# Block attention in a fused fp32 kernel: row maxima in three parts, the first exponential ahead of ScalarE's copies, four probability buffers

## The chip, the cores and the metric

One Trainium2 chip; the program runs on one of its cores. Times are device microseconds (us) of one execution. The kernel before has a median of 3392.8 us over three runs (3386.49 to 3393.48).

## The reference, cut to what matters

The kernel computes two blocks of a network in fp32. Only the attention of the second block is touched by the change: 8 heads, 1024 queries, 1280 keys (256 of a context, 1024 of the sequence), 96 features a head, 64 values a head.

```python
def _block_attention(q, k, v):
    bn, L, H, dk = q.shape
    nb = L // Q_BLOCK
    scale = dk ** -0.5
    qb = q.reshape(bn, nb, Q_BLOCK, H, dk).transpose(1, 0, 2, 3, 4)

    def one(qi):
        s = jnp.einsum('bqhd,bkhd->bhqk', qi, k, preferred_element_type=jnp.float32) * scale
        p = jax.nn.softmax(s, axis=-1).astype(v.dtype)
        return jnp.einsum('bhqk,bkhd->bqhd', p, v)

    o = lax.map(one, qb)
    return o.transpose(1, 0, 2, 3, 4).reshape(bn, L, H * V_DIM)
```

The softmax subtracts the largest score of a row before the exponential; that largest score is what the change computes in another way.

## The kernel before

The function `attend` (L2440) runs in one stretch of the program, between the joint second block and the Fourier mixing. It goes through 32 steps `s`, four (`j` = 0 to 3) for each of 8 heads `h`. A step handles two tiles of 128 query rows, a and b, each with 1280 scores.

PSUM has eight banks of 512 fp32 columns. `pS` takes five: tile a lies in columns 0 to 1279 (sequence keys 0 to 1023 in banks 0 and 1, context keys in the first half of bank 2), tile b in columns 1280 to 2559 (context keys in the second half of bank 2, sequence keys in banks 3 and 4). Two banks, `pt`, are a ring through which everything else goes, and one, `pY`, sums probabilities times values.

The work of a step on each engine, each of which takes its instructions in the order of the program:

- **TensorE** (L2537 to L2640), `pair_scores(s)`: 18 products in three passes each (`scores`, L2555), first a's sequence keys, then the context keys of a and b, then b's sequence keys. The first part waits for exponential a of step s-1, the second for exponential b (`exped`). `scored` is raised twice, after the context part and at the end. Then, for step s-1, `turn_probs` (L2580) transposes the probabilities into the ring in five units t0 to t4 of four 128x128 transposes each; between and behind them come the value sums (`value_sums`, L2593) of two half steps before, four products at a time. At the end of steps j = 0 and 1 the two halves of the next head's queries are made (`make`, L2547), in step j = 2 its keys in three parts (L2552); step j = 3 makes nothing. A ring unit waits until the unit two places before it has been copied out (`wait_free`, L2513): t2 waits for the copy of t0, t3 for that of t1, t4 for that of t2.
- **ScalarE** (L2642 to L2711): copies t0 and t1 of step s-1 out of the ring (L2654), then the two exponentials of step s (L2695), each over 1280 scores with the row sums beside, then the high parts of the made queries or keys (`high`, L2657), and in every second step the copy of half of `pY` (L2706).
- **VectorE** (L2713 to L2813): two maxima over 1280 scores (L2781), one negation and scaling of both columns (L2783), the copies of t2, t3 and t4 (L2728), a reciprocal of both row sums behind exponential b (L2797), then `low` (L2731), which for a query half is five operations from the rotary product at L2739 to L2749, and in every second step the addition at L2808.
- **GpSimd** (L2815 to L2830): multiplies both tiles of probabilities by the reciprocals (L2823). TensorE's t0 waits for it (`normal`).

Steps j = 0 and 2 from the fifth step on end a half of a head's output. Where that head is the second of its pair, the half goes from VectorE's addition over GpSimd's gate (L2830) and ScalarE's copy (L2711) back to VectorE (L2812), in front of the next maxima. This happens in the four steps of heads h = 2, 4 and 6, which finish heads 1, 3 and 5; they are called the odd steps below, the others the even ones.

With three probability buffers (L2490) exponential b of step s goes to the buffer that t4 of step s-1 still reads:

```python
act.wait_ge(biased, s + 1)
if i >= 3:
    act.wait_ge(full, ring[("t", (i - 3) // 2, 4)] + 1)
```

Of the kernel before, what the change touches and what calls it, by code (L numbers as in the profile page):

```python
# [15 lines left out]
ACT = mybir.ActivationFunctionType  # L16
# [2423 lines left out]
def attend(nc, c, t, z, zk, x):  # L2440
# [40 lines left out]
    with Phase(nc, "attn") as ph:  # L2481
# [7 lines left out]
        r1, r2 = ph.sb("turned_cos", (P, HALF)), ph.sb("turned_sin", (P, HALF))  # L2489
        pr = [ph.sb(f"probs{j}", (P, T2)) for j in range(3)]  # L2490
        PT = [ph.sb(f"turned_probs{j}", (P, NKT, HALF)) for j in range(2)]
        yp, ytmp = ph.sb("attended", (P, SEQ)), ph.sb("odd_keys", (P, HALF))
        dg = ph.sb("gate", (P, 4, SEQ))
        mx, nb = ph.sb("max", (P, 2 * NS)), ph.sb("negated_max", (P, 2 * NS))
        sm, ri = ph.sb("sum", (P, 2 * NS)), ph.sb("inverse_sum", (P, 2 * NS))
# [29 lines left out]
        with nc.Block() as block:  # L2525
# [12 lines left out]
            def _(pe):  # L2538
# [24 lines left out]
                def pair_scores(s):  # L2563
# [7 lines left out]
                    scores(h, 2 * j, pS[:, 0:512], 0, 512)  # L2571
                    scores(h, 2 * j, pS[:, 512:1024], 512, 512)
                    if s:
# [6 lines left out]
                def turn_probs(n):  # L2580
                    _, s, i = n
                    o = wait_free(pe, n)
                    for kk in range(2):
                        k = 2 * i + kk
                        for ab in range(2):
                            if kk == 0 and i == 0:
                                pe.wait_ge(normal, 2 * s + ab + 1)
                            c0 = P * k if ab == 0 else (CTX + P * k if k < 8 else P * (k - 8))
                            mm = pe.transpose(o[:, 256 * kk + P * ab:256 * kk + P * ab + P],
                                              pr[(2 * s + ab) % 3][:, c0:c0 + P], c["ident"][:, :])  # L2590
                    mm.then_inc(full, 1)
# [51 lines left out]
            def _(act):  # L2643
# [13 lines left out]
                def high(n):  # L2657
# [7 lines left out]
                    else:  # L2665
                        c0, w = 512 * b, min(512, T2 - 512 * b)
                        act.activation(kh[h % 2][0:NOPE, c0:c0 + w], o[0:NOPE, 0:w], ACT.Copy).then_inc(highs, 1)

                act.wait_ge(landed[0], 80)
                for k in range(QT):  # L2670
# [10 lines left out]
                for s in range(NS + 3):  # L2681
                    if s == 0:
                        for n in values:
                            if n in by_act:
                                move(n)
                    for n in turned_at(s):
                        if n in by_act:
                            move(n)
                    if s < NS:
                        for ab in range(2):  # L2690
                            i = 2 * s + ab
                            act.wait_ge(biased, s + 1)
                            if i >= 3:
                                act.wait_ge(full, ring[("t", (i - 3) // 2, 4)] + 1)
                            act.activation(pr[i % 3][:, :], pS[:, T2 * ab:T2 * (ab + 1)], ACT.Exp, scale=scale,  # L2695
                                           bias=nb[:, i:i + 1], accum_out=sm[:, i:i + 1]).then_inc(exped, 1)
                    for n in made_at(s):
# [16 lines left out]
            def _(dve):  # L2714
# [61 lines left out]
                for s in range(NS + 3):  # L2776
                    if s < NS:
                        for ab in range(2):
                            i = 2 * s + ab
                            dve.wait_ge(scored, i + 1)  # L2780
                            ch.inc(dve.tensor_reduce(mx[:, i:i + 1], pS[:, T2 * ab:T2 * (ab + 1)], AX.X, ALU.max))  # L2781
                        dve.wait_ge(step, ch.n)
                        dve.tensor_scalar(nb[:, 2 * s:2 * s + 2], mx[:, 2 * s:2 * s + 2], -scale, None,  # L2783
                                          ALU.mult).then_inc(biased, 1)
                    if s == 0:
# [30 lines left out]
            def _(pool):  # L2816
                pool.wait_ge(gates_in, 64)
                for s in range(NS + 3):
                    if s < NS:
                        for ab in range(2):  # L2820
                            i = 2 * s + ab
                            pool.wait_ge(inverted, s + 1)
                            pool.tensor_scalar(pr[i % 3][:, :], pr[i % 3][:, :], ri[:, i:i + 1], 1.0, ALU.mult,  # L2823
                                               ALU.mult).then_inc(normal, 1)
# [383 lines left out]
```

## Time and profile before

| what | value |
|---|---|
| median of three runs | 3392.8 us |
| the profiled execution | 3391.3 us, span 3389.5 us |
| attention's 32 steps, first maximum to the end of the last value sums | 2821 to 3198 us of the span |
| mean time from a step's maxima to the next step's | (3173.94 - 2820.95) / 31 = 11.4 us |
| TensorE, VectorE, ScalarE, GpSimd busy, whole span | 93%, 59%, 28%, 4% |
| the same from 2900 to 3000 us | 90%, 69%, 46%, 26% |

The profile page gives busy shares for the whole span, where the large matrix products before attention fill most of it. What bounds attention is read from its own stretch: the waits there, and the timeline of single steps. TensorE's granted clock is given as a share of full speed: 1.00 is 2.4 GHz and 0.50 is 1.2 GHz.

### The profile page before, as it was taken

The page shows a single profiled execution, that of the slowest core. Times are in us where ns is not written, and L with a number is a line of the kernel's source. Part 1 is how long each engine was busy: PE and PEld are TensorE (multiplying, and loading weights), DVE is VectorE, ACT ScalarE, POOL GpSimd, SP SyncE. Part 2 cuts the span into 40 slices and gives each one's busy share as a digit, 9 for nine tenths or more (in the row PEclk, how much of TensorE's full clock was granted, in tenths as well). Part 3 has the DMA queues.
Part 4 walks back from the last instruction along what each step waited for, and adds up shares of the span by engine and source line. Part 5 has one row for each costly group of instructions (what it writes and reads, how often), then busy time and mean ns, then how long its engine had stood idle before and what let it go on. Part 6 is the DMA issues. An engine that isn't in the chain of part 4 may idle for free. (4 is left out here: it accounts for less than half of the span.)

```text
span 3389.5 us, 47701 instructions
## 1 busy us (share of the span) xinstructions
PE 3138.0 (93%) x20182; PEld 2905.0 (86%) x20182; DVE 1991.5 (59%) x2836; ACT 940.7 (28%) x1315; POOL 151.0 (4%) x124
## 2 busy tenths in 40 slices
PE   7999999998887999999999999999898977888787
PEld 7999999998876999999999998999898964555565
DVE  6666777664766455663574466444545526776446
ACT  5221222222444211211111112121323323444323
POOL 0000000000000000000000000000031001222200
PEclk9999999999988999999999999999898988999898
DMA  4223333333374344113213214111121330000121
GB/s 146 87 95 96 94 102 98 108 107 136 119 119 126 110 137 143 51 47 122 75 44 100 94 44 149 51 40 46 56 69 60 135 124 0 1 1 1 73 96 69
DMA packets 101822, 285.74 MB, mean 84 GB/s; under 512 B 13540, under 2 KB 32484, under 8 KB 100328
## 3 DMA queue, kind: packets, MB, share of 16 engines
q1 hardware_dynamic: 101608, 282.69, 26.1%
q8 instruction: 159, 2.61, 0.3%
q14 instruction: 55, 0.45, 0.0%
HBM read 218.79 MB, written 63.85 MB: 83 GB/s over the span
## 5 line engine op out<-in xcount | busy, mean ns | idle before, releaser
L471 PE MATMUL mixer_in_dense<-mix_z_high,mixer_in_whigh 128*128 128x348 f32 x1312 | 431.6, 329 | 15.3 <-DVE mixer_in_wlow L565 10.4
L471 PE MATMUL mixer_in_dense<-mix_z_high,mixer_in_wlow 128*128 128x348 f32 x1312 | 427.2, 326 | 0.0
L471 PE MATMUL mixer_in_dense<-mix_z_low,mixer_in_whigh 128*128 128x348 f32 x1312 | 426.4, 325 | 0.0
L1449 PE MATMUL flow_dense<-rst_norms_operand_b_high,flow_whigh 128*128 128x342 f32 x1248 | 399.5, 320 | 0.4 <-DVE flow_wlow L1542 0.4
L1449 PE MATMUL flow_dense<-irst_norms_operand_b_low,flow_whigh 128*128 128x342 f32 x1248 | 398.6, 319 | 0.0
L1449 PE MATMUL flow_dense<-rst_norms_operand_b_high,flow_wlow 128*128 128x342 f32 x1248 | 397.7, 319 | 0.0
L2012 PE MATMUL joint_dense<-rst_norms_operand_b_high,joint_whigh 128*128 128x342 f32 (+2 forms) x1056 | 344.6, 326 | 18.3 <-DVEq L2129 10.5
L2012 PE MATMUL joint_dense<-rst_norms_operand_b_high,joint_wlow 128*128 128x342 f32 (+2 forms) x1056 | 341.4, 323 | 0.0
L2012 PE MATMUL joint_dense<-irst_norms_operand_b_low,joint_whigh 128*128 128x342 f32 (+2 forms) x1056 | 340.4, 322 | 0.0
L1449 PE MATMUL flow_dense<-first_operand_a_high,flow_whigh 128*128 128x342 f32 (+1 forms) x912 | 291.6, 320 | 17.3 <-DVEq L1563 17.3
L1449 PE MATMUL flow_dense<-first_operand_a_low,flow_whigh 128*128 128x342 f32 (+1 forms) x912 | 292.1, 320 | 0.0
L1449 PE MATMUL flow_dense<-first_operand_a_high,flow_wlow 128*128 128x342 f32 (+1 forms) x912 | 291.4, 320 | 0.0
L471 PEld LDWEIGHTS mixer_in_dense<-mix_z_high,mixer_in_whigh 128*128 128x128 f32 x1312 | 251.6, 192 | 19.6 <-issue 16.9
L471 PEld LDWEIGHTS mixer_in_dense<-mix_z_low,mixer_in_whigh 128*128 128x128 f32 x1312 | 251.1, 191 | 0.0
L471 PEld LDWEIGHTS mixer_in_dense<-mix_z_high,mixer_in_wlow 128*128 128x128 f32 x1312 | 251.0, 191 | 0.0
L1492 ACT ACTIVATE flow_whigh<-first_norms_weights 128x1024 fp32r<-128x1024 f32 (+1 forms) x92 | 95.6, 1039 | 559.9 <-PE flow_dense L1449 536.9
L1449 PEld LDWEIGHTS flow_dense<-rst_norms_operand_b_high,flow_whigh 128*128 128x128 f32 x1248 | 235.3, 189 | 1.3 <-issue 1.2
L1449 PEld LDWEIGHTS flow_dense<-rst_norms_operand_b_high,flow_wlow 128*128 128x128 f32 x1248 | 235.2, 188 | 0.1
L1449 PEld LDWEIGHTS flow_dense<-irst_norms_operand_b_low,flow_whigh 128*128 128x128 f32 x1248 | 234.6, 188 | 0.0
L2012 PEld LDWEIGHTS joint_dense<-rst_norms_operand_b_high,joint_whigh 128*128 128x128 f32 x1056 | 202.0, 191 | 23.9 <-DVEq L2129 8.4
L2012 PEld LDWEIGHTS joint_dense<-rst_norms_operand_b_high,joint_wlow 128*128 128x128 f32 x1056 | 202.6, 192 | 0.6 <-issue 0.5
L2012 PEld LDWEIGHTS joint_dense<-irst_norms_operand_b_low,joint_whigh 128*128 128x128 f32 x1056 | 203.0, 192 | 0.0
(549 smaller groups left out, 5872.3 us busy)
## 6 DMA issues: line engine op xcount, KB each, us to landing
mixer_in_wstage<-w_in SPq DMA_DIRECT2D x56, 512.0 KB, 4.9
mixer_in_mod_w<-w_mod SPq DMA_DIRECT2D x64, 384.0 KB, 3.6
first_norms_weights<-w_up SPq DMA_DIRECT2D x44, 512.0 KB, 3.4
flow_side<-h SPq DMA_DIRECT2D x24, 512.0 KB, 5.1
h<-flow_out SPq DMA_DIRECT2D x24, 512.0 KB, 3.5
first_norms_weights<-ab_w_in SPq DMA_DIRECT2D x20, 512.0 KB, 3.5
p<-mixer_in_out SPq DMA_DIRECT2D x16, 528.0 KB, 2.8
first_norms_weights<-w_down SPq DMA_DIRECT2D x16, 512.0 KB, 3.8
```

The lines of the kernel that those rows point to most:

```text
L471: mm = pe.matmul(bank(s)[:, 0:W], a[n % 2][:, P * m:P * (m + 1)], z[x][:, m, W * b:W * (b + 1)], start=m == 0 and i == 0, stop=m == DT - 1 ...
L1449: mm = pe.matmul(o, w[n % NW][:, P * k:P * (k + 1)], x[h][:, k, where], start=k == 0 and e == 0, stop=k == kt - 1 and e == 2)
L1492: act.activation(wh[n % NW][:, 0:w], stage[n % 2][:, 0:w], ACT.Copy).then_inc(high_ready, 1)
L2012: mm = pe.matmul(pd[s % 2][:, 0:wide], a[n % 2][:, P * k:P * (k + 1)], m, start=k == 0 and e == 0, stop=k == DT - 1 and e == 2)
```

## The change

It is made in `attend` alone, in four parts.

1. `scored` is raised three times a step, so also after a's sequence keys (banks 0 and 1).
2. VectorE takes the maximum of a's 1024 sequence scores, then of both context parts in one instruction (2 x 256 scores into two columns of a new tile `context_max`), then joins, negates and scales for tile a; then the 1024 sequence scores of b, and the same for b. `biased` is raised once a tile instead of once a step.
3. ScalarE runs exponential a before its two copies of t0 and t1, and exponential b behind them.
4. There are four probability buffers, so both exponentials of step s wait only for t4 of step s-2.

```diff
-        pr = [ph.sb(f"probs{j}", (P, T2)) for j in range(3)]
+        pr = [ph.sb(f"probs{j}", (P, T2)) for j in range(4)]
...
-        mx, nb = ph.sb("max", (P, 2 * NS)), ph.sb("negated_max", (P, 2 * NS))
+        mx, mc, nb = (ph.sb(n, (P, 2 * NS)) for n in ("max", "context_max", "negated_max"))
...
-                    scores(h, 2 * j, pS[:, 512:1024], 512, 512)
+                    scores(h, 2 * j, pS[:, 512:1024], 512, 512).then_inc(scored, 1)
...
+                def exponential(s, ab):
+                    i = 2 * s + ab
+                    act.wait_ge(biased, i + 1)
+                    if s >= 2:
+                        act.wait_ge(full, ring[("t", s - 2, 4)] + 1)
+                    act.activation(pr[i % 4][:, :], pS[:, T2 * ab:T2 * (ab + 1)], ACT.Exp, scale=scale,
+                                   bias=nb[:, i:i + 1], accum_out=sm[:, i:i + 1]).then_inc(exped, 1)
...
+                    if s < NS:
+                        exponential(s, 0)
                     for n in turned_at(s):
                         if n in by_act:
                             move(n)
                     if s < NS:
-                        for ab in range(2):
-                            i = 2 * s + ab
-                            act.wait_ge(biased, s + 1)
-                            if i >= 3:
-                                act.wait_ge(full, ring[("t", (i - 3) // 2, 4)] + 1)
...
+                        exponential(s, 1)
...
                         for ab in range(2):
                             i = 2 * s + ab
-                            dve.wait_ge(scored, i + 1)
-                            ch.inc(dve.tensor_reduce(mx[:, i:i + 1], pS[:, T2 * ab:T2 * (ab + 1)], AX.X, ALU.max))
-                        dve.wait_ge(step, ch.n)
-                        dve.tensor_scalar(nb[:, 2 * s:2 * s + 2], mx[:, 2 * s:2 * s + 2], -scale, None,
-                                          ALU.mult).then_inc(biased, 1)
+                            dve.wait_ge(scored, 3 * s + 2 * ab + 1)
+                            c0 = (T2 + CTX) * ab
+                            ch.inc(dve.tensor_reduce(mx[:, i:i + 1], pS[:, c0:c0 + SEQ], AX.X, ALU.max))
+                            if ab == 0:
+                                dve.wait_ge(scored, 3 * s + 2)
+                                ch.inc(dve.tensor_reduce(mc[:, i:i + 2], pS[:, SEQ:SEQ + 2 * CTX].rearrange(
+                                    "p (a x) -> p a x", a=2), AX.X, ALU.max))
+                            dve.wait_ge(step, ch.n)
+                            dve.tensor_scalar(nb[:, i:i + 1], mx[:, i:i + 1], mc[:, i:i + 1], -scale, ALU.max,
+                                              ALU.mult).then_inc(biased, 1)
```

The indices of `pr` in the transposes and on GpSimd change from % 3 to % 4 with it.

On ScalarE, from the copies of a step that begins a head to the end of its third step (L2654 copies of t0 and t1, L2695 and in the change L2674 the exponentials, L2662 and L2664 the high parts of queries, L2667 those of keys), before:

```order
731 L2654 ACTIVATE attn_turned_probs<-attn_turned 128x2x256 x2
732 L2695 ACTIVATE attn_probs,attn_sum<-attn_scores,attn_negated_max 128x1280 x2
733 L2662 ACTIVATE attn_query_high<-attn_turned 64x512
734 L2664 ACTIVATE attn_query_high<-attn_turned_cos 32x512
735 L2654 ACTIVATE attn_turned_probs<-attn_turned 128x2x256 x2
736 L2695 ACTIVATE attn_probs,attn_sum<-attn_scores,attn_negated_max 128x1280 x2
737 L2667 ACTIVATE attn_key_high<-attn_turned 64x512 x2
738 L2667 ACTIVATE attn_key_high<-attn_turned 64x256
```

and with the change:

```order
734 L2674 ACTIVATE attn_probs,attn_sum<-attn_scores,attn_negated_max 128x1280
735 L2654 ACTIVATE attn_turned_probs<-attn_turned 128x2x256 x2
736 L2674 ACTIVATE attn_probs,attn_sum<-attn_scores,attn_negated_max 128x1280
737 L2662 ACTIVATE attn_query_high<-attn_turned 64x512
738 L2664 ACTIVATE attn_query_high<-attn_turned_cos 32x512
739 L2674 ACTIVATE attn_probs,attn_sum<-attn_scores,attn_negated_max 128x1280
740 L2654 ACTIVATE attn_turned_probs<-attn_turned 128x2x256 x2
741 L2674 ACTIVATE attn_probs,attn_sum<-attn_scores,attn_negated_max 128x1280
742 L2667 ACTIVATE attn_key_high<-attn_turned 64x512 x2
743 L2667 ACTIVATE attn_key_high<-attn_turned 64x256
```

The pair of copies stood ahead of both exponentials; now it stands between them.

On VectorE, a step's maxima and what follows them up to the reciprocal, before:

```order
1953 L2781 TENSOR_REDUCE attn_max<-attn_scores 128x1 x2
1954 L2783 TENSOR_SCALAR attn_negated_max<-attn_max 128x2
1955 L2728 COPY attn_turned_probs<-attn_turned 128x2x256 x3
1956 L2797 RECIPROCAL attn_inverse_sum<-attn_sum 128x2
1957 L2739 TENSOR_TENSOR attn_turned_sin<-attn_turned,attn_turn 32x512
```

and with the change:

```order
1965 L2786 TENSOR_REDUCE attn_max<-attn_scores 128x1
1966 L2789 TENSOR_REDUCE attn_context_max<-attn_scores 128x2
1967 L2792 TENSOR_SCALAR attn_negated_max<-attn_max,attn_context_max 128x1
1968 L2786 TENSOR_REDUCE attn_max<-attn_scores 128x1
1969 L2792 TENSOR_SCALAR attn_negated_max<-attn_max,attn_context_max 128x1
1970 L2732 COPY attn_turned_probs<-attn_turned 128x2x256 x3
1971 L2806 RECIPROCAL attn_inverse_sum<-attn_sum 128x2
1972 L2743 TENSOR_TENSOR attn_turned_sin<-attn_turned,attn_turn 32x512
```

Three instructions have become five, with the first negation behind the second of them; copies and reciprocal keep their places. TensorE's instructions keep their order.

## Rows read from the trace of the kernel before

**Rows 1.** Stretches: busy time (and instructions) of each engine, TensorE's clock, DMA.

```profile
core 0: us, PE busy (x) PEld busy (x) DVE busy (x) ACT busy (x) POOL busy (x), PEclk, DMA share, GB/s
2900.00:3000.00 100.00, 90.11 (x448) 53.67 (x447) 69.46 (x95) 46.04 (x76) 26.36 (x20) 1.00 0.00 1
```

**Rows 2.** Waits from 2822 to 3190: us in total, times, longest.

```profile
ACT attn_probs L2695 <- PE attn_turned L2589: 22.3, 14, 1.7
```

**Rows 3.** Groups by line and shape: busy us, mean ns, idle before.

```profile
L2781 DVE TENSOR_REDUCE attn_max<-attn_scores 128x1 f32<-128x1280 f32 x64 | 92.5, 1485 | 17.2 <-PE attn_scores L2559 16.7
...
L2728 DVE COPY attn_turned_probs<-attn_turned 128x512 f32<-128x512 f32 x96 | 63.3, 688 | 37.3 <-PE attn_turned L2589 37.2
```

**Rows 4.** Timeline, a step j = 1: start, duration, instruction [idle before].

```profile
2971.31 0.70 DVE L2739 TENSOR_TENSOR attn_turned_sin<-attn_turned,attn_turn 32x512 f32<-32x512 f32 x1 [1.25 <-PE attn_turned L2547]
...
2975.13 0.68 DVE L2808 TENSOR_TENSOR attn_attended<-attn_values_sum,attn_odd_keys 64x512 f32<-64x512 f32 x1
...
2975.74 2.87 DVE L2781 TENSOR_REDUCE attn_max<-attn_scores 128x1 f32<-128x1280 f32 x2
...
2976.88 1.09 PE L2589 MATMUL attn_turned<-all_ident,attn_probs 128*128 128x128 f32 x8
...
2977.90 1.08 PE L2606 MATMUL attn_values_sum<-attn_turned_probs,attn_values 128*64 128x512 f32 x4
...
2978.85 1.33 ACT L2695 ACTIVATE attn_probs<-attn_scores,attn_negated_max 128x1280 f32<-128x1280 f32 x1 [2.54 <-DVE attn_negated_max L2783]
...
2979.48 0.66 PE L2589 MATMUL attn_turned<-all_ident,attn_probs 128*128 128x128 f32 x4 [0.50 <-DVE attn_turned_probs L2728]
...
2980.07 1.99 PE L2547 MATMUL attn_turned<-attn_cq,attn_wq 128*128 128x512 f32 x4
...
2980.23 1.33 ACT L2695 ACTIVATE attn_probs<-attn_scores,attn_negated_max 128x1280 f32<-128x1280 f32 x1
...
2982.09 0.70 DVE L2739 TENSOR_TENSOR attn_turned_sin<-attn_turned,attn_turn 32x512 f32<-32x512 f32 x1 [0.25 <-PE attn_turned L2547]
...
2986.82 2.89 DVE L2781 TENSOR_REDUCE attn_max<-attn_scores 128x1 f32<-128x1280 f32 x2
```

**Rows 5.** Timeline, ScalarE's two copies and the exponential behind them.

```profile
2964.32 1.09 ACT L2654 ACTIVATE attn_turned_probs<-attn_turned 128x512 f32<-128x512 f32 x2 [3.59 <-PE attn_turned L2589]
...
2965.29 1.33 ACT L2695 ACTIVATE attn_probs<-attn_scores,attn_negated_max 128x1280 f32<-128x1280 f32 x1
```

**Rows 6.** Timeline, a step j = 3 and the start of the next head.

```profile
2997.51 2.89 DVE L2781 TENSOR_REDUCE attn_max<-attn_scores 128x1 f32<-128x1280 f32 x2 [0.57 <-PE attn_scores L2559]
...
3002.71 0.66 PE L2589 MATMUL attn_turned<-all_ident,attn_probs 128*128 128x128 f32 x4
...
3004.36 0.39 PE L2559 MATMUL attn_scores<-attn_key_low,attn_query_high 96*128 96x512 f32 x1
3004.94 0.38 PE L2559 MATMUL attn_scores<-attn_key_high,attn_query_high 96*128 96x256 f32 x1 [0.18 <-ACT attn_probs L2695]
...
3005.95 2.89 DVE L2781 TENSOR_REDUCE attn_max<-attn_scores 128x1 f32<-128x1280 f32 x2 [0.87 <-PE attn_scores L2559]
...
3007.88 0.98 PE L2589 MATMUL attn_turned<-all_ident,attn_probs 128*128 128x128 f32 x7 [0.47 <-POOL attn_probs L2823]
```

**Rows 7.** Timeline, a step j = 1 and a step j = 3, both odd.

```profile
3022.52 1.14 PE L2589 MATMUL attn_turned<-all_ident,attn_probs 128*128 128x128 f32 x8 [1.42 <-ACT attn_turned_probs L2654]
...
3022.74 2.89 DVE L2781 TENSOR_REDUCE attn_max<-attn_scores 128x1 f32<-128x1280 f32 x2
...
3046.77 2.89 DVE L2781 TENSOR_REDUCE attn_max<-attn_scores 128x1 f32<-128x1280 f32 x2
```

**Rows 8.** Timeline behind the last step: TensorE after its longest idle time in attention.

```profile
3183.07 0.44 PE L2589 MATMUL attn_turned<-all_ident,attn_probs 128*128 128x128 f32 x1 [3.28 <-POOL attn_probs L2823]
3184.29 1.75 PE L2589 MATMUL attn_turned<-all_ident,attn_probs 128*128 128x128 f32 x7 [0.77 <-POOL attn_probs L2823]
3185.97 1.98 PE L2606 MATMUL attn_values_sum<-attn_turned_probs,attn_values 128*64 128x512 f32 x4
```

**Rows 9.** Stretches, the same place, columns as in rows 1.

```profile
3183.00:3186.00 3.00, 2.16 (x10) 1.56 (x10) 0.00 (x0) 0.60 (x1) 1.23 (x1) 0.50 0.00 0
```

More of the change, by code:

```diff
@@ L2589, in turn_probs @@
                             mm = pe.transpose(o[:, 256 * kk + P * ab:256 * kk + P * ab + P],
-                                              pr[(2 * s + ab) % 3][:, c0:c0 + P], c["ident"][:, :])
+                                              pr[(2 * s + ab) % 4][:, c0:c0 + P], c["ident"][:, :])
                     mm.then_inc(full, 1)
@@ L2689, in _ @@
                     if s < NS:
-                        for ab in range(2):
-                            i = 2 * s + ab
-                            act.wait_ge(biased, s + 1)
-                            if i >= 3:
-                                act.wait_ge(full, ring[("t", (i - 3) // 2, 4)] + 1)
-                            act.activation(pr[i % 3][:, :], pS[:, T2 * ab:T2 * (ab + 1)], ACT.Exp, scale=scale,
-                                           bias=nb[:, i:i + 1], accum_out=sm[:, i:i + 1]).then_inc(exped, 1)
+                        exponential(s, 1)
                     for n in made_at(s):
@@ L2822, in _ @@
                             pool.wait_ge(inverted, s + 1)
-                            pool.tensor_scalar(pr[i % 3][:, :], pr[i % 3][:, :], ri[:, i:i + 1], 1.0, ALU.mult,
+                            pool.tensor_scalar(pr[i % 4][:, :], pr[i % 4][:, :], ri[:, i:i + 1], 1.0, ALU.mult,
                                                ALU.mult).then_inc(normal, 1)
```

## The prediction

> **What bounds the kernel now.** I read the stretches first, since only attention changes. From 2900 to 3000 us TensorE is busy 90 of 100 us at the full clock, VectorE 69 [rows 1]. So TensorE's idle time, about 10% of 353 us or 35 us, is the most that any reordering could win, and no engine is full: the steps are bound by a loop through several engines. The waits give one piece of it, ScalarE's wait for t4 of the step before, 22.3 us in 14 steps [rows 2], which is the buffer that the change adds. Whether that wait matters is read from the timeline of single steps.
>
> Measure a step from M, the start of its maxima. In a step j = 1, M is 2975.74 and VectorE came to it straight from other work [rows 4]. The loop is: exponential a at M+3.11; t2 and t3 on TensorE at M+1.14; four value products at M+2.16; t4 at M+3.74, late by 0.50 because VectorE's copy of t2 stands behind the maxima; the next query half at M+4.33; VectorE's `low` at M+6.35, with 0.25 of idle time for that query half; the next maxima at M+11.08, again with no wait for scores. The next M is set by `low`, and `low` by t4 and the query half. TensorE's scores are ready by then. Step j = 2 is alike, with keys in place of queries: its M is 2986.82, the next one 2997.51, where VectorE idled 0.57 [rows 4, 6]. Step j = 3 is bound by TensorE: VectorE idles 0.87 before 3005.95, and M to M is 8.44 [rows 6].
>
> So there are two kinds of step. In those that TensorE bounds, earlier maxima and exponentials can help. In those that VectorE enters late, ScalarE has its copies of t0 and t1 done long before M, and waits 2.54 for the negation [rows 4].
>
> **Maxima in parts.** 1280 scores take 1485 ns and a 512-wide copy from PSUM 688 ns [rows 3], so 768 more columns cost 797 ns: 1.04 ns each and 155 ns fixed. From M to exponential a are now 3.11 us, with 2560 columns, two reductions and a negation [rows 4]. After the change the way holds 1536 columns, two reductions and a negation: 1024 x 1.04 = 1.06 less, so M+2.05. For both tiles together VectorE gets one reduction (155 ns fixed) and one negation more, about 0.3 a step or 10 us in all. I cost that at nothing: it lies behind the first negation, and VectorE has nothing to copy until ScalarE has freed t2's bank, below. Were the cover gone, it would cost up to 10 us. The Trainium skill (VectorE: DVE Perf Modes, "The TRN2 errata") speaks against such a split, because many small tiles pay the fixed part each. Its table has 120 cycles at 0.96 GHz for an operation that reads PSUM and 58 for one that does not, an estimate of 0.19 a step and 6 us in all in place of 10.
>
> **The earlier signal.** The sixth score product ended at 3004.75 and the maxima began at 3005.95 [rows 6]. With a signal there the first maximum can begin at about 3004.79, 1.16 earlier, where VectorE is waiting. Where VectorE comes late it brings nothing.
>
> **ScalarE's order.** Now t2 must wait for: M, 2.05 to exponential a, 1.38 from one exponential to the next instruction (2978.85 to 2980.23 [rows 4]), the first copy. Two copies take 1.09, the next instruction starts 0.97 after the first, so one copy ends at 0.60 [rows 5]; with 0.04 for the hand-over t2 starts at 2.05 + 1.38 + 0.60 + 0.04 = M+4.07, not M+1.14. Then by rows 4: 1.02 for t2 and t3, 1.08 for the value products, 0.59 for t4, 2.02 from the query half to `low`: M+8.78, not M+6.35. `low` itself took 4.73 (2982.09 to 2986.82); where it does not run beside GpSimd it took 3.82 (2971.31 to 2975.13) [rows 4]. GpSimd would be nearly done by then, so I take 3.82: next M at +12.60, against 11.08.
>
> Step by step:
> - j = 1, seven steps: +1.52 each, 10.6.
> - j = 2: t4 and all behind it 2.43 later. Four even ones lose that less the 0.57 of idle time [rows 6], 1.86 each; three odd ones have no such idle time: 4 x 1.86 + 3 x 2.43 = 14.7.
> - j = 3, even: t4 at 4.07 + 1.02 + 1.08 = M+6.17; from t4 to the earlier signal are 3004.79 - 3002.71 = 2.08 [rows 6]: 8.25 in place of 8.44, -0.2 each, four times. Odd: VectorE enters late as in j = 1 (the one at 3046.77 [rows 7]), so t4 is 2.4 later and only the 1.16 comes off: +1.2, three times. Together 2.9.
> - j = 0, six steps (the first step of all is left as it is): the first maximum lies 1.16 nearer to the scores, while `low` keeps its place in TensorE's order; off come the wait for exponential b (0.18 of idle, 0.35 to 0.45 of delay) and about 0.4 of GpSimd's 0.47 [rows 6]. +0.3 each, 1.9.
> - The last head makes nothing; its steps are bound by TensorE and gain 0.2 to 0.5 each: -1.1.
>
> **The fourth buffer**: exponential b would start at 2.05 + 1.38 + 0.97 = M+4.40, and now starts at M+4.49 [rows 4, 5]. Its stall goes, but what comes late next is t4's copy, behind which the reciprocal stands. So nothing beyond the small gains above.
>
> Sum at a full clock: 10.6 + 14.7 + 2.9 + 1.9 - 1.1 = **+29 us**.
>
> **The clock.** TensorE would now be idle before t2. In j = 1 the gap is 4.07 - 1.14 = 2.93; in odd steps it grows from 1.42 by 4.07 + 0.22 to 5.7, three times [rows 4, 7]. Behind the last step TensorE idled 3.28 and 0.77, and the granted clock was then 0.50, the lower level [rows 8, 9]: seven transposes took 1.75 in place of 0.98, four value products 1.98 in place of 1.08 [rows 4, 6, 8]. A fall costs 1.7 us in these alone, and they are on the loop. The three long gaps surely pay it. Some 14 gaps of about 3 us are left. The stretch of [rows 1] stayed at 1.00 all along, and [rows 7] show that gaps of 1.42 occur now, the end of attention lost it behind 3.28 and 0.77; what I have to price lies between, so I take half of them. 10 x 1.7 = 17. Bounds: 3 x 1.7 = 5, and 17 x 1.7 = 29, or 36 at 2.1 if the work behind is slow too.
>
> **Forecast**: 29 + 17 = 46 us on 3391.3, the profiled execution, which is 1.5 below the median; on the median 3392.8 + 46 = 3439, with 3425 to 3452 as this case's own range.
>
> **Rivals.**
> 1. *The clock holds.* If gaps of 3 us do not lower it and the long ones hardly, the sum is 29: 3422, from 3412. For it: the gaps before odd t2 are at full speed now.
> 2. *The clock falls in every gap, and longer.* 29 + 29 to 29 + 36, rounded up for slow query products: 3451 to 3465. The Trainium skill (TensorE: Matmul & The Clock Gate, "HAM oscillation") describes this: a kernel whose matmuls came in bursts with waits between them fell back at every burst. [...] The fall at the end of attention agrees with it; no row of before has a gap of 2.9.
> 3. *Faster: TensorE bounds every step.* The late t2 would be absorbed if 4.71 us of work from t2 to `low` fitted in front of `low`'s other condition, exponential b and the reciprocal, at M+6.35; that decides at t2 = M+1.64. Then `low` keeps its time, and only the gains remain: 0.1 a step, and 0.5 to 0.9 in the dozen steps where TensorE waits for exponential b or GpSimd. That is -10, 3383. Against it: t2 cannot start before ScalarE has run an exponential that cannot start before M+2.
> 4. *No change.* Gains of rival 3 and a partial loss cancel, or ScalarE's copies are not on the path in most steps: within 7 us, 3393.
>
> **How the numbers follow.** About 0.2%, or 7 us, is what a measurement of this kernel can tell from no change. Forecast 0.48, rival 1 0.16, rival 2 0.20, rival 3 0.09, rival 4 0.07. Faster is rival 3, 0.09; same is rival 4, 0.07; slower the rest, 0.84. The range reaches from rival 1's lower end to rival 2's upper end, 3412 to 3465; rivals 3 and 4 are left out (0.16), and a little of both ends.
>
> **What would show it.** The waits after: TensorE's t2 on ScalarE's copy, near zero on TensorE now but for odd steps, should be the largest, some 2.9 a time. ScalarE's wait for t4 should be gone, and GpSimd's hold on t0 be shorter. Exponential a at M+2.05 and t2 at M+4.07 in every step. M to M: 12.6 in j = 1 and 12.5 in even j = 2 steps, 8.25 in even j = 3. The clock in stretches of 5 us behind long gaps tells between the forecast and rivals 1 and 2. Wrong would be: t2 ahead of exponential a's end, or j = 1 steps that keep 11.1 us.

## The result and the profile after

The changed kernel takes 3445.4 us (median of four runs, 3443.98 to 3449.6), the kernel before, timed beside it, 3390.0 us: a ratio of 1.0166, 95% interval 1.0148 to 1.0183, so 1.7% slower. The forecast was 3439 us and a loss of 46 us; the loss is 55.

The profiled execution of the change took 3449.6 us, the longest of its four. It entered attention 7.1 us later than that of before (the last activation of the stage ahead starts at 2772.20 against 2765.10), in code that the change does not touch; that is spread between executions. From there to the last subtraction of attention it took 487.0 us against 436.3: the change costs 51 us inside attention in these two traces.

Stretches, columns as in [rows 1]:

```profile
core 0: us, PE busy (x) PEld busy (x) DVE busy (x) ACT busy (x) POOL busy (x), PEclk, DMA share, GB/s
2900.00:3000.00 100.00, 84.22 (x392) 50.35 (x390) 60.68 (x97) 37.41 (x62) 23.70 (x18) 0.91 0.00 1
```

TensorE is busy 84 of 100 us where it was 90 [rows 1], although part of that work now runs at half the clock: the granted clock is 0.91 on average where it was 1.00. All other engines do less in the same time as well.

The waits in attention, us in total, times, longest:

```profile
ACT attn_probs L2674 <- DVE attn_negated_max L2792: 109.7, 31, 6.1
DVE attn_turned_probs L2732 <- PE attn_turned L2589: 87.0, 75, 2.3
PEld attn_turned L2589 <- ACT attn_turned_probs L2654: 84.3, 31, 6.6
PE attn_turned L2589 <- ACT attn_turned_probs L2654: 58.2, 18, 5.7
```

ScalarE no longer waits for t4, the 22.3 us of [rows 2]. In its place TensorE waits 58 us in 18 places for ScalarE's copies of t0 and t1, which stand behind an exponential that itself waits for the maxima.

Timeline of an even step j = 1, the same step s = 13 as in [rows 4]; start, duration, instruction [idle before]:

```profile
3000.25 1.21 DVE L2786 TENSOR_REDUCE attn_max<-attn_scores 128x1 f32<-128x1024 f32 x1
...
3001.38 0.67 DVE L2789 TENSOR_REDUCE attn_context_max<-attn_scores 128x2 f32<-128x512 f32 x1
3002.09 0.21 DVE L2792 TENSOR_SCALAR attn_negated_max<-attn_max,attn_context_max 128x1 f32<-128x1 f32 x1
...
3002.33 1.33 ACT L2674 ACTIVATE attn_probs<-attn_scores,attn_negated_max 128x1280 f32<-128x1280 f32 x1 [3.05 <-DVE attn_negated_max L2792]
...
3003.65 1.07 ACT L2654 ACTIVATE attn_turned_probs<-attn_turned 128x512 f32<-128x512 f32 x2
...
3004.29 1.60 PE L2589 MATMUL attn_turned<-all_ident,attn_probs 128*128 128x128 f32 x8 [2.83 <-ACT attn_turned_probs L2654]
...
3005.82 1.97 PE L2606 MATMUL attn_values_sum<-attn_turned_probs,attn_values 128*64 128x512 f32 x4
...
3007.72 0.88 PE L2589 MATMUL attn_turned<-all_ident,attn_probs 128*128 128x128 f32 x4
...
3010.36 0.69 DVE L2743 TENSOR_TENSOR attn_turned_sin<-attn_turned,attn_turn 32x512 f32<-32x512 f32 x1 [0.95 <-PE attn_turned L2547]
...
3014.37 1.23 DVE L2786 TENSOR_REDUCE attn_max<-attn_scores 128x1 f32<-128x1024 f32 x1
```

M is 3000.25. Exponential a starts at M+2.08 (it was M+3.11), so the maxima in parts do bring it forward by 1.03 us. The copies follow at M+3.40, and t2 starts at M+4.04, behind 2.83 us of idle time; it was M+1.14. Value products at M+5.57, t4 at M+7.47, `low` at M+10.11, the next maxima at M+14.12 against M+11.08.

The stretches around it show the clock fall:

```profile
3002.00:3004.29 2.29, 0.00 (x0) 0.00 (x1) 1.61 (x4) 1.96 (x4) 0.00 (x0) 1.00 0.00 0
3004.29:3007.72 3.43, 3.43 (x12) 1.43 (x13) 1.38 (x2) 1.74 (x3) 0.00 (x0) 0.58 0.00 0
3007.72:3012.00 4.28, 4.28 (x20) 3.06 (x19) 2.34 (x5) 0.59 (x1) 2.50 (x2) 0.94 0.00 0
```

In the gap it is still 1.00; in the 3.43 us after it, over t2, t3 and the value products, it is 0.58, so mostly 0.50, the lower level of 1.2 GHz. The products that take 1.08 us at full speed [rows 4] take 1.97.

### The profile page after: what moved, and what is told of

It reads as the page before. It is cut to its first block and busy times, and to the rows that moved or that the text cites. A ratio compares the mean times of both kernels' runs of the same rounds, so it can differ in the third digit from the quotient of the medians.

```text
span 3447.8 us, 47764 instructions
## 1 busy us (share of the span) xinstructions
PE 3164.5 (92%) x20182; PEld 2922.9 (85%) x20182; DVE 1997.8 (58%) x2900; ACT 935.3 (27%) x1315; POOL 151.0 (4%) x124
## 5 line engine op out<-in xcount | busy, mean ns | idle before, releaser
L2012 PE MATMUL joint_dense<-rst_norms_operand_b_high,joint_whigh 128*128 128x342 f32 (+2 forms) x1056 | 344.1, 326 | 19.4 <-DVEq L2129 10.5
L471 PEld LDWEIGHTS mixer_in_dense<-mix_z_high,mixer_in_whigh 128*128 128x128 f32 x1312 | 253.2, 193 | 19.5 <-issue 16.8
```

The source lines that it names most:

```text
L471: mm = pe.matmul(bank(s)[:, 0:W], a[n % 2][:, P * m:P * (m + 1)], z[x][:, m, W * b:W * (b + 1)], start=m == 0 and i == 0, stop=m == DT - 1 ...
L2012: mm = pe.matmul(pd[s % 2][:, 0:wide], a[n % 2][:, P * k:P * (k + 1)], m, start=k == 0 and e == 0, stop=k == DT - 1 and e == 2)
```

## The experiments

The theory: in the steps that VectorE enters late, ScalarE's copies of t0 and t1 behind exponential a hold t2, and with it everything up to the next maxima (29 us at a full clock); TensorE's idle time in front of t2 lowers the clock, which costs the rest. The rivals: the split maxima cost (by their fixed parts or by shared banks), the fourth buffer costs, or the order costs alike in every step. Nine kernels besides the change were timed. The kernel before was timed again beside them, with medians of 3389.9 us beside E1 to E4, 3391.9 beside E5 to E8 and 3388.5 beside E9, so small differences between runs of different groups are judged by the ratios.

| run | what | median us | ratio to before, 95% interval |
|---|---|---|---|
| E1 | the change with ScalarE's old order | 3385.0 | 0.9984, 0.9975 to 0.9994 |
| E2 | the new order alone | 3504.8 | 1.0345, 1.0328 to 1.0363 |
| E3 | four buffers alone | 3385.3 | 0.9986, 0.9978 to 0.9995 |
| E4 | maxima in parts alone | 3400.1 | 1.0029, 1.0016 to 1.0043 |
| E5 | the change, TensorE kept busy, fillers too long | 3444.2 | 1.0150, 1.0132 to 1.0168 |
| E6 | E1 and early copies in j = 2 | 3380.8 | 0.9970, 0.9958 to 0.9983 |
| E7 | E6 and late output halves | 3368.6 | 0.9930, 0.9916 to 0.9945 |
| E8 | the new order only where TensorE bounds | 3386.9 | 0.9984, 0.9973 to 0.9994 |
| E9 | the change, TensorE kept busy, fewer fillers | 3416.9 | 1.0083, 1.0052 to 1.0115 |

The time from a step's M to the next, read off the timelines as the difference of the starts of the first maxima (a cell stands for steps that agree within 0.1 us unless a range is given; steps 4 to 27):

| steps | before | forecast at full clock | change | E9 | E1 | E7 |
|---|---|---|---|---|---|---|
| j = 0 even | 13.9 | 14.2 | 14.20 | 14.20 | 14.19 | 14.2 to 14.6 |
| j = 0 odd | 16.8 | 17.1 | 17.05 | 17.06 | 17.04 | 14.31 |
| j = 1 even | 11.08 | 12.6 | 14.14 | 12.56 | 10.53 | 10.53 |
| j = 1 odd | 11.10 | 12.6 | 14.77 | 12.60 | 10.5 to 11.4 | 10.89 |
| j = 2 even | 10.69 | 12.55 | 13.8 to 14.0 | 12.46 | 10.4 | 9.9 |
| j = 2 odd | 12.9 to 13.0 | 15.4 | 16.9 | 15.32 | 13.3 to 13.4 | 9.85 |
| j = 3 even | 8.44 | 8.25 | 8.20 | 8.21 | 7.93 | 7.93 |
| j = 3 odd | 7.06 | 8.3 | 9.80 | 8.22 | 6.18 | 7.8 |

**E1: the old order back.**

```diff
-                    if s < NS:
-                        exponential(s, 0)
                     for n in turned_at(s):
                         if n in by_act:
                             move(n)
                     if s < NS:
+                        exponential(s, 0)
                         exponential(s, 1)
```

> The change without its part 3: ScalarE copies t0 and t1 ahead of both exponentials, as before; maxima in parts and four buffers stay. Theory (the order on ScalarE is the loss, and through it the clock): t2 starts again right behind the first value products, the clock stays at 1.00, M to M is about 11.3 in steps j = 1 (+0.3 from the longer maxima ahead of the copy of t2), and steps bound by TensorE gain 0.5 to 1; in all about 7 us under the kernel before, 3383. Rival A (the split maxima cost, in fixed parts or by sharing PSUM banks with TensorE and ScalarE): 10 to 50 us above before. Rival B (the fourth buffer or its place in SBUF costs): above before as well.

3385.0 us, 5 us under before and 60 under the change: with the old order the whole loss is gone, and both rivals, on maxima and on buffers, fall. The gain was a little smaller than expected, 5 us for 7, and it did not come where it was expected: even j = 1 steps took 10.53, not 11.3. The timeline of step s = 13 shows where the time went.

```profile
2978.76 1.21 DVE L2785 TENSOR_REDUCE attn_max<-attn_scores 128x1 f32<-128x1024 f32 x1
...
2982.85 0.65 PE L2589 MATMUL attn_turned<-all_ident,attn_probs 128*128 128x128 f32 x4 [0.84 <-DVE attn_turned_probs L2731]
...
2984.40 2.65 POOL L2831 TENSOR_SCALAR attn_probs<-attn_probs,attn_inverse_sum 128x1280 f32<-128x1280 f32 x2 [9.49 <-DVE attn_inverse_sum L2805]
...
2986.92 0.68 DVE L2744 TENSOR_TENSOR attn_turned_cos<-attn_turned_cos,attn_turned_sin 32x512 f32<-32x512 f32 x1
```

t4 is late by 0.84, more than the 0.50 of [rows 4], as the longer maxima ahead of its bank's copy would have it: M+4.09 against M+3.74. But GpSimd starts at M+5.64 and has 0.13 left, to M+8.29, when VectorE comes to the sum of the two rotary products at M+8.16. That operation, of which all operands lie in SBUF, takes 0.68 there. Before, it started at 2983.55, while GpSimd worked from 2981.94 to 2984.59, and took 1.58, to 0.54 behind GpSimd's end:

```profile
2981.94 2.65 POOL L2823 TENSOR_SCALAR attn_probs<-attn_probs,attn_inverse_sum 128x1280 f32<-128x1280 f32 x2 [9.15 <-DVE attn_inverse_sum L2797]
...
2983.55 1.58 DVE L2741 TENSOR_TENSOR attn_turned_cos<-attn_turned_cos,attn_turned_sin 32x512 f32<-32x512 f32 x1
```

The 0.90 saved here outweighs the 0.35 by which t4 is later: 11.08 + 0.35 - 0.90 = 10.53. In the table one odd j = 1 step of E1 took 11.4 instead of 10.5. In that step the granted clock fell, to 0.68 over 4.2 us from t4 on; in the two others it stayed at 1.00.

**E2: the new order alone**, on the kernel before, with its three buffers and whole maxima; the edit is that of the change's third part, with `biased` waited for at `s + 1` and the wait for t4 as before.

```diff
+                    if s < NS:
+                        exponential(s, 0)
                     for n in turned_at(s):
                         if n in by_act:
                             move(n)
                     if s < NS:
-                        for ab in range(2):
...
+                        exponential(s, 1)
```

> The kernel before with part 3 alone: exponential a ahead of the copies of t0 and t1, whole maxima, three buffers. Theory: exponential a at M+3.11, so t2 at M+5.1, about 1.1 later than in the change; exponential b then waits for t4, so the reciprocal and the next scores come late too. M to M about 15 in steps j = 1, 10 in steps j = 3; in all 80 to 100 us above before, about 3480: worse than the change, whose other parts soften it. Rivals A and B (maxima or buffers are the loss): within 7 us of before.

3504.8 us, 115 above before. The direction and the order of the runs are as the theory has it, but the loss is 15 us above the upper end of the expected 80 to 100. A step j = 1:

```profile
3021.10 2.87 DVE L2785 TENSOR_REDUCE attn_max<-attn_scores 128x1 f32<-128x1280 f32 x2
...
3024.21 1.33 ACT L2674 ACTIVATE attn_probs<-attn_scores,attn_negated_max 128x1280 f32<-128x1280 f32 x1 [4.07 <-DVE attn_negated_max L2787]
...
3026.17 1.92 PE L2589 MATMUL attn_turned<-all_ident,attn_probs 128*128 128x128 f32 x8 [3.86 <-ACT attn_turned_probs L2654]
...
3030.59 1.33 ACT L2674 ACTIVATE attn_probs<-attn_scores,attn_negated_max 128x1280 f32<-128x1280 f32 x1 [3.98 <-PE attn_turned L2589]
...
3032.30 2.65 POOL L2827 TENSOR_SCALAR attn_probs<-attn_probs,attn_inverse_sum 128x1280 f32<-128x1280 f32 x2 [14.13 <-DVE attn_inverse_sum L2801]
...
3033.70 1.79 DVE L2745 TENSOR_TENSOR attn_turned_cos<-attn_turned_cos,attn_turned_sin 32x512 f32<-32x512 f32 x1
```

Exponential a at M+3.11 and t2 at M+5.07 are as expected; exponential b is 3.98 late for t4. The estimate had counted neither the clock, which is granted at 0.51 in the 3.4 us behind this t2, nor the rotary sum beside GpSimd, 1.79 for 0.68. M to M is 16.05 to 16.08 in even j = 1 steps. So parts 1, 2 and 4 together save in this order: with them it costs 55, without them 115.

**E3: four buffers alone.** `range(3)` and all `% 3` become 4, and the wait is for t4 of step s-2.

```diff
-                            if i >= 3:
-                                act.wait_ge(full, ring[("t", (i - 3) // 2, 4)] + 1)
+                            if s >= 2:
+                                act.wait_ge(full, ring[("t", s - 2, 4)] + 1)
```

> The kernel before with part 4 alone: four probability buffers. Theory: exponential b starts at M+1.4 behind exponential a in every step, ScalarE's 22 us of waiting for t4 are gone, and with them TensorE's wait for exponential b and most of its wait for GpSimd in the steps it bounds, 0.8 to 1.2 us a head and some in the last head: 8 to 10 us under before, 3381. Rival (that wait is off the path): within 3 us of before.

3385.3 us, 5 us under before, where 8 to 10 were expected and 3 would have been the rival's. The buffer is worth half of the forecast. Even j = 3 steps take 8.0 in place of 8.44, and odd j = 0 steps 16.3 in place of 16.8; the even j = 0 steps win 0.46 in one head and 0.08 in two, and even j = 1 steps under 0.1. So the wait was on the path in steps that TensorE bounds, and not in all of them. The profiled executions show a second reason. All gains together are 5.1 us, but steps of the odd heads lost 1.8 us of it: odd j = 1 steps took 11.8, 11.7 and 11.1 where they had taken 11.1, and the j = 2 step behind the last of them 13.4 for 12.9. TensorE idles 1.42 us just ahead of such a j = 1 step and 1.82 in it, as before, but the clock stayed up before and fell here. Behind the second gap of step s = 9, before:

```profile
2934.44:2938.00 3.56, 3.56 (x13) 2.23 (x14) 2.31 (x5) 2.77 (x5) 1.09 (x1) 1.00 0.00 0
```

and in E3:

```profile
2934.40:2938.00 3.60, 3.60 (x9) 1.87 (x9) 1.40 (x3) 2.10 (x4) 1.20 (x1) 0.57 0.00 0
```

**E4: maxima in parts alone**, with three buffers and the old order.

```diff
-        pr = [ph.sb(f"probs{j}", (P, T2)) for j in range(4)]
+        pr = [ph.sb(f"probs{j}", (P, T2)) for j in range(3)]
...
-                    if s >= 2:
-                        act.wait_ge(full, ring[("t", s - 2, 4)] + 1)
+                    if i >= 3:
+                        act.wait_ge(full, ring[("t", (i - 3) // 2, 4)] + 1)
```

(against E1, with the indices of `pr` back at % 3)

> The kernel before with parts 1 and 2 alone: maxima in three parts, two negations, three buffers, old order. Theory: VectorE's extra 0.3 a step delays the copy of t2 in the 14 steps that it enters late, and the earlier signal brings little while exponential b waits for t4: 0 to 5 us above before, 3394. Rival A (the split maxima carry the loss): 20 us or more above before.

3400.1 us, 10 above before: worse than the 0 to 5 of the theory, well short of its rival. From its waits:

```profile
ACT attn_probs L2674 <- PE attn_turned L2589: 47.1, 31, 1.7
```

This is the wait of [rows 2], now in all 31 steps: exponential a ends earlier, and exponential b still has to wait for t4. By steps, the loss sits mainly in j = 0, 1.0 us each (14.9 even, 17.7 odd), and 0.35 in even j = 1; from step 4 on even j = 2 and all j = 3 steps are 0.3 to 0.7 shorter. With the fourth buffer (E1) the j = 0 steps take 14.2 and 17.0, so 0.7 of the 1.0 goes with the buffer's wait and only the rest can be VectorE's extra work. With the buffer the split makes no difference in time, 3385.0 us (E1) against 3385.3 (E3). VectorE's extra work can be read from the change's trace: the three reductions have means of 1220, 679 and 1220 ns and the negations 214 each, 3.55 us together against 2 x 1.485 + 0.17 = 3.14 before. That is 0.41 a step, more than the 0.3 that the prediction took, and more than double the 0.19 that it worked out from the table of the Trainium skill (VectorE: DVE Perf Modes, "The TRN2 errata"); the page's point, that many small tiles pay the fixed part each, stands.

**E8: the new order only where TensorE bounds.**

```diff
+                    ahead = s % 4 == 0 or s >= NS - 4 or (s % 4 == 3 and s // 4 % 2)
+                    ahead = ahead or s // 4 == 0 and s % 4 == 3
-                    if s < NS:
+                    if s < NS and ahead:
                         exponential(s, 0)
                     for n in turned_at(s):
                         if n in by_act:
                             move(n)
+                    if s < NS and not ahead:
+                        exponential(s, 0)
```

> The changed kernel with exponential a ahead of the copies only in the steps that TensorE bounds (all j = 0, even j = 3, the last head), and behind them in the 17 others. Theory: the loss sits in the others only, so this is E1 plus 0 to 3 us, about 3386, M to M 14.2 in j = 0 and 8.2 in even j = 3 as in the changed kernel, 10.5 in j = 1. Rival (the order costs in every step alike): a third to a half of the loss stays, 3405 to 3420.

3386.9 us, by the ratio the same as E1. Even j = 3 steps take 8.20 as in the change, 0.27 more than in E1, and even j = 0 steps 14.20 as in both. So all but some 2 us of the harm is done in the 17 steps that VectorE enters late, and the new order helps in none of the others.

**E5: TensorE kept busy in the gaps.** A zero matrix times the values is added to the running sum in `pY`, which leaves it as it is.

```diff
+                def keep_busy(s):
+                    if s < 4 or s >= 28:
+                        return
+                    odd = (s // 4) % 2 == 0
+                    n = {0: 0, 1: 10 if odd else 5, 2: 5, 3: 5 if odd else 0}[s % 4]
+                    for k in range(n):
+                        pe.matmul(pY[0:VD, :], zero[:, :], V[:, k % NKT, :], start=False, stop=False,
+                                  skip_group_check=True)
...
                         if n[2] % 2 and H is not None:
                             value_sums(H, pairs[n[2] // 2:n[2] // 2 + 1])
+                        if n[2] == 1:
+                            keep_busy(s)
```

> The changed kernel with extra value products of a zero matrix (they add 0 to the running sum, so the result stays) on TensorE in the gap in front of t2: 5 in steps j = 1 and 2 and odd j = 3, 10 in odd j = 1, none elsewhere. They fill most of a gap but not all. Theory (the clock falls in these gaps, and that is the part of the loss above the 29 us): granted clock near 1.00 in attention, M to M back to 12.6 in even j = 1, 12.5 in even j = 2, 8.3 in odd j = 3; 20 to 25 us under the changed kernel, about 3422. Rival (the excess has another cause, such as shared PSUM banks): M to M stays 14.1 and 14.0, and the time is that of the changed kernel or more.

3444.2 us, hardly a gain: taken by itself, the outcome of the rival. The stretches and the timeline say that it is not.

```profile
3000.00:3100.00 100.00, 98.14 (x434) 53.00 (x433) 60.92 (x97) 36.81 (x61) 20.65 (x16) 1.00 0.00 1
```

```profile
3003.82 1.21 DVE L2800 TENSOR_REDUCE attn_max<-attn_scores 128x1 f32<-128x1024 f32 x1
...
3004.86 4.45 PE L2601 MATMUL attn_values_sum<-attn_values,attn_zero 128*64 128x512 f32 x10
...
3009.25 1.09 PE L2591 MATMUL attn_turned<-all_ident,attn_probs 128*128 128x128 f32 x8
```

The clock stayed at 1.00, but a filler takes not the 0.5 us that I had planned with but 0.86 (two matmuls at 0.43 each), so five of them held t2 to M+5.43. From there on the step ran at full speed: 13.89 is the 12.6 of the theory and 1.3 of too long a filler. The fillers were too many, and E9 repeats the experiment with fewer.

**E9: fewer fillers.**

```diff
-                    n = {0: 0, 1: 10 if odd else 5, 2: 5, 3: 5 if odd else 0}[s % 4]
+                    n = {0: 0, 1: 6 if odd else 3, 2: 3, 3: 3 if odd else 0}[s % 4]
```

> As E5 with fewer fillers. One took 0.86 us on TensorE, not the 0.5 that E5 was laid out for, so its five lasted 4.3 us and held t2 to M+5.43. Now 3 (2.6 us) in steps j = 1, 2 and odd j = 3, and 6 (5.2 us) in odd j = 1: all end before ScalarE frees t2's bank at about M+4.04. Theory (the clock is the excess over 29 us): granted clock 1.00, t2 at M+4.04 at full speed, M to M 12.5 to 12.6 in even j = 1 and j = 2, 8.3 in odd j = 3; about 22 us under the changed kernel, 3422. Rival (something else slows TensorE or VectorE): M to M of 13 or more although t2 starts in time.

3416.9 us, 28.5 under the change, the ratio to before is 1.0083. The clock:

```profile
2900.00:3000.00 100.00, 96.49 (x447) 53.63 (x444) 64.76 (x105) 41.15 (x68) 23.78 (x18) 1.00 0.00 1
```

and step s = 13, with M at 2987.41:

```profile
2991.45 1.15 PE L2591 MATMUL attn_turned<-all_ident,attn_probs 128*128 128x128 f32 x8 [0.27 <-ACT attn_turned_probs L2668]
...
2992.53 1.08 PE L2617 MATMUL attn_values_sum<-attn_turned_probs,attn_values 128*64 128x512 f32 x4
...
2993.54 0.66 PE L2591 MATMUL attn_turned<-all_ident,attn_probs 128*128 128x128 f32 x4
...
2995.95 0.69 DVE L2757 TENSOR_TENSOR attn_turned_sin<-attn_turned,attn_turn 32x512 f32<-32x512 f32 x1 [0.96 <-PE attn_turned L2549]
...
2999.98 1.23 DVE L2800 TENSOR_REDUCE attn_max<-attn_scores 128x1 f32<-128x1024 f32 x1
```

t2 starts at M+4.04 as in the change, but it, t3 and the products take 2.09 in place of 3.43, and the next maxima come at M+12.57 in place of M+14.12. TensorE does more work than in the change and the kernel is faster. This separates the two parts of the loss: about 28 us remain without the falls from step 5 on, and those falls are the other 27. The first fillers stand in step 5. In steps 1 and 2 E9 idles 3.6 us before t2 as the change does, and the granted clock behind is 0.60 and 0.69 over 3.3 us; the kernel before has one fall there, in step 1. So the 28 us still hold one fall more than the kernel before.

**E6 and E7: toward a version that beats both.** Both keep the old order, the split maxima and the four buffers of E1. E6 lets VectorE copy t2 and t3 between tile a's negation and tile b's maximum in the steps j = 2:

```diff
+                            if ab == 0 and early(s):
+                                for n in turned_at(s)[2:4]:
+                                    move(n)
```

with `early(s)` true for j = 2 outside the last head.

> E1 (old order, maxima in parts, four buffers) and in steps j = 2 VectorE copies t2 and t3 between tile a's negation and tile b's maximum. Theory: t4 there waits only for VectorE's copy of t2 (0.57 us of idle time in front of it); it goes, exponential b still ends before the keys are there, so M to M in j = 2 falls from 10.4 to about 9.8 and the whole by 4 us: 3381. Rival (exponential b, now later, takes its place): no change from E1, 3385.

3380.8 us, as expected; even j = 2 steps fell from 10.4 to 9.9, where 9.8 was expected. The gain over E1 is not clear of noise, since the intervals of the two ratios overlap, and in the profiled executions two odd j = 1 steps in which the clock fell (11.9 and 11.7 for 10.5) took much of it back. If it is real, the split of the maxima pays here for the first time, since it makes a place to put the copies.

E7 takes the detour over GpSimd's gate out of the way of the next maxima:

```diff
                         if h % 2:
-                            e = 2 * (h // 2) + H % 2
-                            dve.wait_ge(y_high, e + 1)
-                            tt(x[1][:, h // 2, at], yp[:, at], x[0][:, h // 2, at].bitcast(F32),
-                               ALU.subtract).then_inc(y_low, 1)
+                            late.append((h, H))
...
                         dve.reciprocal(ri[:, 2 * s:2 * s + 2], sm[:, 2 * s:2 * s + 2]).then_inc(inverted, 1)
+                    finish()
```

where `finish` holds the lines taken out; on ScalarE the copy to `x[0]` goes the same way, to behind the next step's copies of t0 and t1. A last `finish()` stands behind the loop.

> E6 and, in the odd steps, ScalarE's copy of a finished output half stands behind the next step's copies of t0 and t1, and VectorE's subtraction for it behind the next reciprocal, so that neither waits for GpSimd's gate in front of the maxima. Theory (VectorE's entry into the maxima sets the loop): M to M in odd j = 0 falls from 17.0 to about 14.3, in odd j = 2 from 13.3 to about 10.2, odd j = 3 rises from 6.2 to 7.9; about 12 us under E6, 3369. Rival (TensorE bounds these steps anyway): within 3 us of E6.

3368.6 us, 0.7% under before (ratio 0.9930, interval 0.9916 to 0.9945), 12 under E6 and 77 under the change. Odd j = 0 steps went from 17.04 to 14.31, odd j = 2 from 13.3 to 9.85, odd j = 3 rose from 6.18 to 7.8, each within 0.4 of what was expected. It is the fastest version of the study.

```profile
2900.00:3000.00 100.00, 95.72 (x496) 58.92 (x496) 75.12 (x121) 48.17 (x80) 27.30 (x21) 1.00 0.00 1
```

TensorE is now busy 96 of 100 us at the full clock, without fillers, so a better order of the same work could win no more than the other 4 of 100.

## Why the prediction was right, point by point

- **What bounds the kernel.** The loop of a late step over exponential a, ScalarE's copy, t2, t4, the query half and `low` is what the runs show. E1 and E8 confine the loss, but for some 2 us, to ScalarE's order in the steps that VectorE enters late. E7 confirms the same reading from the other side: one wait less ahead of VectorE's maxima in six steps (j = 0 and 2 of the odd heads) gave 12 us. The loss itself rules out rivals 3 and 4, and the falls of the clock rule out rival 1.
- **Exponential a at M+2.05, t2 at M+4.07.** Measured 2.08 and 4.04 in step s = 13, and 2.09 to 2.11 and 4.04 to 4.12 in all others but the first.
- **The sum at a full clock, +29 us.** E9 is the kernel nearest to that sum, 28 us over before, of which one fall of the clock in step 2, some 1.7 us by the price below (an estimate), does not belong to a full clock. So the part at a full clock is nearer 26 us, 3 under the forecast. By kinds of steps, the forecast of 12.6, 12.55, 15.4, 8.25 and 8.3 us stands against 12.56 to 12.60, 12.46, 15.32, 8.21 and 8.22; j = 0 steps got 0.3 longer, as forecast, and the last head's three 1.0 us shorter together, for 1.1. Within a step j = 1 two terms were off and cancelled, which was luck. In E9's step s = 13 from t2 to `low` are 4.50 us where the sum had 4.71, and `low` takes 4.03 where it had 3.82. The 3.82 was read as the time without GpSimd beside it. In truth GpSimd was at work then too, from 2970.15 to 2972.79, but it ended just as the rotary sum began (2972.76). What makes `low` longer is that one sum: 0.88 in E9, 0.68 there.
- **The clock, +17 us.** Here the size was off, and the term is the count of falls. I took ten at 1.7 us, half of the shorter gaps. In the change's trace the clock fell behind all 17, the idle times being 2.56 to 5.70 us and the granted clock in the 3.4 us behind them 0.50 to 0.62. For the 15 from step 5 on E9 gives the price: the change exceeds E9 by 1.3 to 1.6 in even j = 1 steps, in all j = 2 steps and in odd j = 3, and by 2.2 in odd j = 1; together 25 us. The price of 1.7 was right on average, the choice of half was wrong. Rival 2 had all falls and 58 to 65 us in all; with 55 the result lies between the forecast and it, and its mechanism, every gap, is what happened. So the forecast hit its range with too few falls. The case told in the Trainium skill (TensorE: Matmul & The Clock Gate, "HAM oscillation"), a fall at every burst, agrees with this trace. The waits in that case are given as about 3 to 5 us; nine of the 17 here were shorter, 2.56 to 2.84, and the clock fell behind them as well. The prediction said that no row of before has a gap of 2.9. None that it shows has, but the trace holds one just ahead of the first step:

```profile
2810.25:2813.11 2.86, 0.01 (x1) 0.01 (x1) 2.53 (x4) 0.83 (x2) 0.00 (x0) 1.00 0.00 0
2813.11:2815.80 2.69, 2.65 (x4) 0.47 (x4) 1.76 (x3) 0.97 (x2) 0.00 (x0) 0.57 0.00 0
```

There TensorE had worked only 1.07 us since an idle time of 1.04, so the case is not quite the same, but it pointed to rival 2.

- **Maxima in parts at nothing.** In the change VectorE waits 87 us for TensorE's transposes, so the cover was there, and the sum at a full clock comes out without a price for the split. The prediction's "up to 10 us" without the cover and E4's 10 us agree in the number only: most of E4's loss sits in j = 0 steps and goes with the wait for t4, which that 10 us did not mean. The extra work itself was mis-sized, 0.41 us a step and not 0.3.
- **The fourth buffer, nothing beyond small gains.** Alone it is worth 5 us (E3), which the prediction had not given. In the change the wait it removes would have been dearer: E2 without it and without the split loses 60 us more. How much of these 60 is the buffer's and how much the split's was not tried.
- **The total.** 46 forecast, 55 measured, of which 51 in attention in the profiled pair. The other four are not explained by any step of the working; the executions of the change alone spread over 5.6 us.

## What to carry to other kernels

Before an instruction that waits is moved ahead of one that is ready, look at who waits for the ready one. Here 1 us was won on an exponential and 3 us lost on a copy behind it, since the copy frees the bank that the busiest engine needs. Where an engine is late, take work away from in front of it (E7), and count a new idle time on TensorE twice, once as time and, where it is as long as those here (2.56 us and more), once as clock.

## What the runs showed of the hardware that was not expected

- The granted clock fell behind gaps of only 2.56 to 2.84 us in all nine steps of that kind (3.43 us at 0.58 after 2.83 us idle), though TensorE had worked for 11 us or more without a gap of 0.9 us.
- Shorter gaps went either way. Behind 1.42 us of idle time, 2.15 of work and 1.82 of idle time the clock stayed at 1.00 three times before and fell three times in E3 (0.57, 0.63 and 0.72 over 3.5 us). So a clock that held in one profiled execution does not show that such gaps are safe.
- Matmuls that add nothing to the result made the kernel faster, 28 us in E9. They must end before the gap does: in E5, where they lasted 1.4 us too long, they gave nearly everything back. Where the gap can be closed instead, that is better: E1 has the old order, no fillers, and is 32 us faster than E9.
- VectorE's rotary sum, with all operands in SBUF, took 0.68 us alone, 1.58 when it started during GpSimd's multiplication, and 1.79 in E2. It waits rather than runs slower: in all eleven traces, wherever it took over 0.75 us, it ended 0.53 to 0.54 us behind the end of the GpSimd instruction that ran at its start. The rotary products, with one operand in PSUM, took 0.69 to 0.70 beside GpSimd and without it. So the moment at which GpSimd starts decides up to 1.1 us of a step, though no semaphore makes VectorE wait for it here.
